# Queries before keys and values, keys and values between the attention blocks, decode beside the output projection

## The chip, the cores and the metric

The program runs on one core of a Trainium2 chip. A core has a matrix engine (TensorE, in profiles PE, its weight loads PEld), three engines that work on 128 partitions in parallel (VectorE or DVE, ScalarE or ACT, GpSimd or POOL), and a queue that only issues transfers (SyncE or SP). They run side by side and wait for each other through semaphores. Data lies in device memory, in SBUF (128 partitions) or in PSUM (8 banks of 512 float32 a partition, the only place TensorE writes). The metric is the time of one execution on the device, in microseconds.

## The reference, cut to what matters

One step of a two-layer decoder over a prompt of 1024 tokens and 8 sample tokens, 1032 rows of width 1024, all in float32. Layer 0 is a gated linear recurrence (untouched here). After its FFN, keys and values are projected once and the second layer attends to them:

```python
x = x + swiglu_ffn(rmsnorm(x, norm_ffn[0]), ...)            # end of layer 0
k_sh, v_sh = split(rmsnorm(x, kv_norm) @ w_kv, 2)            # 1024 -> 2048, also outputs
q = rmsnorm(x, norm_mix[1]) @ w_q_b                          # 4 heads x 2 maps x 128
s = einsum(q, k) * scale + rel_bias[bucket(q_pos - k_pos)]   # prompt: causal, 8 blocks of 128
p = softmax(s);  a = p[map 0] - lam * p[map 1]
o = rmsnorm(a @ v, subln) * (1 - lam_init)                   # per head, 256 values
x = x + o @ w_out_b
x = x + swiglu_ffn(rmsnorm(x, norm_ffn[1]), ...)
```

The 8 sample tokens do the same over 256 cached keys and values each, which lie in pages that a page table names, and their own new ones.

## The kernel before, in words

Rows are held feature-major: `resid` (X) is 8 chunks of 128 features by 1032 tokens. Each float32 projection is done as three products of a rounded part and a rest: `split_product` (L647) issues hi*hi, lo*hi and hi*lo on TensorE. The operands are `act_hi` and `act_lo` (XH, XL, written by ScalarE and VectorE) and `w_hi` and `w_lo`, which GpSimd's `split` (L591) makes from a slab of 2048 columns a partition in `w_stage`. There is one stage buffer and there are two slots of slabs: SyncE's `slab` (L454) refills the stage when the last split is done (`w_split`), and a split begins when TensorE has retired the slot two slabs back (`w_used`). A slab feeds 144 products on 344 columns (three token tiles).

Between layer 0's FFN and layer 1's FFN the kernel runs in phases with a barrier of TensorE, ScalarE and VectorE between them (`barrier`, L453): "f0", "kv", "q", "attn", "dattn".
- Last down pair of the FFN (`add_pair`): VectorE adds 24 results to X, ScalarE squares each chunk, VectorE sums.
- `norm("kv")`: sums over partitions, reciprocal root, then VectorE scales each chunk (`act_whole`, L1678), ScalarE rounds it, VectorE takes the rest (`act_lo`, L1676). X is spilled to device memory, since its place is used.
- `kv_slabs`: 16 chunks of 128 key or value features; ScalarE copies them out of PSUM, TensorE turns them to token rows (`turn_chunk`), VectorE copies the rows, ScalarE's queue writes them out. All keys (`k_feat`) and values (`v_rows`) stay in SBUF.
- `projection("q")`: the spilled X comes back in part, is scaled with another gain and split again, 4 slabs.
- Attention: 4 heads by 8 query blocks, an item being one block of one head. TensorE runs scores one item ahead, values one item behind; VectorE makes logits with bias and their maximum, ScalarE exponentials, VectorE the difference of the two maps, TensorE turns it, ScalarE copies it (`a_tok`), TensorE multiplies by the values. Scores use PSUM banks 0 to 3, turned weights 4 and 5, values 6, turned rows 7. The order within an item is written out in `at_head` on each engine. The rows of a head are normalised one head later.
- Decode ("dattn"): each sample token's query is spread over partitions by TensorE; VectorE multiplies it with the first page of keys, GpSimd with the second; VectorE reduces both. Softmax, then 64 products of value pages (256 columns each) against a memset block of weight columns.
- Output projection: 24 groups over the first 6 chunks (`out_early`), then 24 over the last 2 (`out_late`), added to the reloaded X; chunks of the next FFN's operand follow (`finish_projection`).

Of the kernel before, what the change touches and what calls it, by code (L numbers as in the profile page):

```python
# [80 lines left out]
def build(nc, i, o):  # L81
    ctx = ExitStack()
    with ctx:
# [44 lines left out]
        VS = place("v_s", [P, DEC])  # L128
        FS = place("f_s", [P, DEC])
        DL = place("chunk_decay", [P, NB])  # L130
# [16 lines left out]
        w_hi = sem("w_hi")  # L147
        phase_done = sem("phase_done")
# [12 lines left out]
        x_back = sem("x_back")  # L161
# [3 lines left out]
        chunk_turned = sem("chunk_turned")  # L165
        proj_free = sem("proj_free")
        rows_ready = sem("rows_ready")
        chunk_kept = sem("chunk_kept")
        rows_out = sem("rows_out")
# [43 lines left out]
        woa_free = sem("woa_free")  # L213
        wob_full = sem("wob_full")
# [24 lines left out]
        at_qb = sem("at_qb")  # L239
# [12 lines left out]
        d_bias = sem("d_bias")  # L252
        d_prod = sem("d_prod")
        dq_full = sem("dq_full")
        d_products = sem("d_products")
        d_products1 = sem("d_products1")
        dq_copied = sem("dq_copied")
        d_zeros = sem("d_zeros")
        d_orows = sem("d_orows")
        d_o_full = sem("d_o_full")  # L260
        d_a = sem("d_a")
        d_diag = sem("d_diag")
        d_o = sem("d_o")
        d_ss = sem("d_ss")
        d_rel = sem("d_rel")
# [3 lines left out]
        d_logit_full = sem("d_logit_full")  # L269
        d_bias_full = sem("d_bias_full")  # L270
        d_weights = sem("d_weights")
        d_a_full = sem("d_a_full")
        d_sq = sem("d_sq")
        d_ss_full = sem("d_ss_full")
        d_max = sem("d_max")
        d_exp = sem("d_exp")
        d_at = sem("d_at")
        d_ss_sum = sem("d_ss_sum")
        d_rstd = sem("d_rstd")
# [30 lines left out]


        S_HG, S_WOA, S_F0 = 0, 16, 21
        EARLY = 6
        S_K = S_F0 + 3 * NPAIR
        S_V, S_Q, S_WOB, S_F1 = S_K + 4, S_K + 8, S_K + 12, S_K + 17
# [6 lines left out]
        def part(name, shape, dt=F32):  # L322
# [33 lines left out]
        KT = part("k_feat", [P, C, SEQ])  # L356
        VTOK = part("v_rows", [P, NB, D])
        SF = at("kv_chunk", [P, T], F32, x_at)
        TKS = at("k_rows", [P, NB, P], F32, x_at + T * 4)
        TSS = at("kv_rows_sample", [DEC, P], F32, x_at + T * 4 + 4096)  # L360
        KV_CHUNKS = -(-(T * 4 + 4096 + P * 4) // (T * 4))
        QA = at("q_all", [P, C, T], F32, x_at)

        PB = [at(f"probs{s}", [P, 2, SEQ], F32, xh_at + s * 8192) for s in range(2)]
        BT = at("near_bias", [P, AH, 256], F32, xh_at + 16384)
        AT = at("a_tok", [P, NB, P], F32, xh_at + 20480)
        QB = [at(f"q_block{s}", [P, 2, P], F32, xh_at + 24576 + s * 1024) for s in range(2)]

        OT = ([at(f"o_tok{n}", [P, 256], F32, xh_at + 26624 + n * 1024) for n in range(6)]
              + [at(f"o_tok{n}", [P, 256], F32, rs_at + (n - 6) * 1024) for n in (6, 7)])  # L370
        OSQ = at("o_square", [P, 256], F32, rs_at + 2048)
        HK = at("hankel", [P, AH, 256], F32, xh_at + 8192)
        OH = at("onehots", [NBUCKET + 1, 384 + PAST + 1], F32, xh_at)
        RBX = at("rel_rows", [NBUCKET + 1, AH], F32, xh_at + 4096)
        DR = at("dist_vals", [AH, 384], F32, xh_at + 4352)


        empty = S_WOB % 2 ^ 1
        KPG = [[at(f"k_page{s}{g}", [P, D], F32, w_slots_at + (2 * s + empty) * SLAB * 4 + g * D * 4) for g in range(2)]
               for s in range(2)]  # L380
        VPG = [[at(f"v_page{s}{g}", [P, D], F32, arena + (4 + 2 * s + g) * 4096) for g in range(2)] for s in range(4)]
        KQP = [at(f"d_k_times_q{g}", [P, C, P], F32, xh_at + g * 4096) for g in range(NPG)]
        QBC = [at(f"d_q_all{s}", [P, C, P], F32, arena + s * 4096) for s in range(2)]

        WZ = at("d_weight_cols", [P, NPG, 32, 63], F32, xh_at + 8192)
        ORW = at("d_o_rows", [32, 256], F32, xh_at + 8192 + NPG * 32 * 63 * 4)
        d0 = arena + 12 * 4096
# [4 lines left out]
        DAT = at("d_a_tok", [P, 2, 64], F32, d0 + 4608)  # L392
        DDG = at("d_diag", [64, 64], F32, d0 + 5632)
# [9 lines left out]
        DST = at("d_stats", [64, 8], F32, d0 + 10880)  # L403

# [5 lines left out]
        PHASES = ["loaded", "f0", "kv", "q", "attn", "dattn"]  # L410
# [3 lines left out]
        SCALINGS = ["mix0", "woa", "ffn0", "kv", "q", "wob", "ffn1"]  # L414
        WHOLE = ["mix0", "kv", "q"]
        OLD = ["mix0", "kv"]
        LATE = ["ffn0", "ffn1"]
        PROJECTIONS = ["woa", "k", "v", "q", "wob"]
# [14 lines left out]
        AT_LATE = [(), (0, 1)] + [(n,) for n in range(2, NB)]  # L433
# [4 lines left out]

        def at_item(h, n, ahead):

            return h + (n + ahead) // NB, (n + ahead) % NB
# [11 lines left out]
        def _(sp):  # L453
# [62 lines left out]
            square(S_K, 8, i["w_kv"])  # L516
            square(S_Q, 4, i["w_q_b"][0])
            out_early(S_WOB, i["w_out_b"][0], 0, 1)

# [12 lines left out]
            for s in range(2):  # L532
                pages(kc, KPG, k_page_in, 0, s, s)
# [1579 lines left out]
```

## Time and profile before

| | us |
|---|---|
| median of 3 runs | 3135.26 (3132.32 to 3135.92) |
| profiled execution | 3135.91, span 3134.2 |
| TensorE busy in the span | 2867.7 (91%) |
| VectorE, ScalarE, GpSimd busy | 1300.4, 602.5, 923.0 |
| mean granted TensorE clock | 0.954 |

The span runs from the first to the last instruction of the profiled execution; what lies around it is 1.7 us. Busy times overlap between engines. A matmul's shown duration holds its way through the array too: one on 344 columns is shown as 326 ns, but the next starts 157 ns after it. Granted clock 1.00 is 2.4 GHz, 0.50 is 1.2 GHz.

### The profile page before, as it was taken

What the parts mean: (1) busy time and instruction counts of PE and PEld (TensorE: products, weight loads), DVE (VectorE), ACT (ScalarE), POOL (GpSimd) and SP (SyncE); (2) the same over time, 40 slices, a digit from 0 to 9 for tenths busy, and PEclk for the clock granted to TensorE, in tenths of its full rate; (3) what the DMA queues carried; (4) which work ended last, traced back from release to release, by engine and by line L of the source; (5) the groups of instructions that cost most, each with busy time, mean ns of one, the idle gap of its engine ahead of it and who ended that gap; (6) DMA issues with size and microseconds to landing.
All of it is one profiled execution on the core that took longest, in us unless ns stands there. A gap on an engine that the chain in (4) does not pass through costs nothing.

```text
span 3134.2 us, 43595 instructions
## 1 busy us (share of the span) xinstructions
PE 2867.7 (91%) x17823; PEld 2757.0 (88%) x17823; DVE 1300.4 (41%) x2092; ACT 602.5 (19%) x1113; POOL 923.0 (29%) x264
## 2 busy tenths in 40 slices
PE   5999999989899999999899796676698999999998
PEld 4999999989899999999799794444498999999998
DVE  6345555554433333333621305565234333333335
ACT  3122222212200000000221113453112000000003
POOL 3322222222343333334223320002133434333331
PEclk7999999989999999999999898897799999999999
DMA  3111111121111111111222201003311111111111
GB/s 95 40 43 51 54 55 56 42 89 42 41 41 54 41 54 41 54 41 48 88 75 81 95 24 35 0 0 122 141 51 41 41 54 41 54 41 54 41 54 55
DMA packets 196055, 170.23 MB, mean 54 GB/s; under 512 B 5514, under 2 KB 181373, under 8 KB 195502
## 3 DMA queue, kind: packets, MB, share of 16 engines
q1 hardware_dynamic: 157728, 132.20, 13.6%
q10 hardware_dynamic: 38158, 35.50, 3.4%
q8 instruction: 140, 2.29, 0.3%
q14 instruction: 29, 0.24, 0.0%
HBM read 142.35 MB, written 25.33 MB: 54 GB/s over the span
## 4 chain that ended last, share of the span: by engine, by line
PE 78%; issue 11%; DVE 8%; DMA 1%; POOL 1%; ACT 1%; SPq 0%; ACTq 0%; DVEq 0%; POOLq 0%
PE ps L649 23%; PE ps L651 23%; PE ps L650 23%; PE ps L860 3%; DVE act_whole L1678 1%; DVE hg_k L1763 1%; PE ps L1148 1%; DVE act_lo L1676 1%; DVE act_lo L1714 1%; DVE rstd L1693 1%; DMA k_page<-in_cache_k 1%; DVE hg_q L1762 1%; POOL d_k_times_q L633 1%; DVE act_lo L1698 1%; DVE act_whole L1641 0%
## 5 line engine op out<-in xcount | busy, mean ns | idle before, releaser
L649 PE MATMUL ps<-act_hi,w_hi 128*128 128x344 f32 x3840 | 1253.7, 326 | 71.9 <-DVE act_lo L1676 48.5
L650 PE MATMUL ps<-act_lo,w_hi 128*128 128x344 f32 x3840 | 1237.3, 322 | 0.0
L651 PE MATMUL ps<-act_hi,w_lo 128*128 128x344 f32 x3840 | 1237.0, 322 | 0.0
L597 POOL TENSOR_TENSOR w_hi<-w_stage,ones 128x2048 fp32r<-128x2048 f32 (+1 forms) x104 | 378.0, 3634 | 1520.9 <-PEq L701 1513.1
L649 PEld LDWEIGHTS ps<-act_hi,w_hi 128*128 128x128 f32 x3840 | 731.4, 190 | 81.2 <-issue 56.8
L650 PEld LDWEIGHTS ps<-act_lo,w_hi 128*128 128x128 f32 x3840 | 731.4, 190 | 1.7 <-issue 1.0
L651 PEld LDWEIGHTS ps<-act_hi,w_lo 128*128 128x128 f32 x3840 | 730.9, 190 | 0.0
L599 POOL TENSOR_TENSOR w_lo<-w_stage,w_hi 128x2048 fp32r<-128x2048 f32 (+1 forms) x104 | 477.0, 4587 | 8.2
L1878 DVE TENSOR_TENSOR resid<-resid,ps 128x344 f32<-128x344 f32 x528 | 270.6, 513 | 185.7 <-PE ps L651 185.2
L649 PE MATMUL ps<-h_hi,w_hi 128*128 128x344 f32 x1056 | 339.1, 321 | 1.4 <-DVE resid L1878 1.4
L651 PE MATMUL ps<-h_hi,w_lo 128*128 128x344 f32 x1056 | 338.3, 320 | 0.0
L650 PE MATMUL ps<-h_lo,w_hi 128*128 128x344 f32 x1056 | 338.1, 320 | 0.0
L1855 DVE TENSOR_TENSOR ps<-ps,rstd 128x344 f32<-128x344 f32 x132 | 68.9, 525 | 391.4 <-PE ps L651 391.4
L1858 DVE TENSOR_TENSOR ps<-ps,rstd 128x344 f32<-128x344 f32 x132 | 69.3, 525 | 363.2 <-PE ps L651 363.2
L1428 ACT ACTIVATE silu_gate<-ps 128x344 f32<-128x344 f32 x132 | 60.4, 458 | 807.7 <-DVE ps L1855 807.7
L649 PEld LDWEIGHTS ps<-h_hi,w_hi 128*128 128x128 f32 x1056 | 198.8, 188 | 4.5 <-DVE resid L1878 4.2
L650 PEld LDWEIGHTS ps<-h_lo,w_hi 128*128 128x128 f32 x1056 | 198.7, 188 | 0.0
L651 PEld LDWEIGHTS ps<-h_hi,w_lo 128*128 128x128 f32 x1056 | 198.6, 188 | 0.0
L1433 ACT CAST h_hi<-ps 128x344 fp32r<-128x344 f32 x132 | 59.0, 447 | 445.8 <-DVE ps L1861 445.8
L860 PEld LDWEIGHTS ps<-hg_q,hg_k 128*128 128x128 f32 x896 | 111.3, 200 | 25.9 <-DVE hg_k L1763 25.1
L860 PE MATMUL ps<-hg_q,hg_k 128*128 128x64 f32 x896 | 113.9, 282 | 20.9 <-DVE hg_k L1763 20.9
L1083 PE MATMUL ps<-v_rows,a_tok 128*128 128x256 f32 (+1 forms) x288 | 78.4, 422 | 44.1 <-ACT a_tok L1511 44.0
(251 smaller groups left out, 2234.2 us busy)
## 6 DMA issues: line engine op xcount, KB each, us to landing
w_stage<-in_w_gate_up SPq DMA_DIRECT2D x88, 512.0 KB, 5.0
w_stage<-in_w_down SPq DMA_DIRECT2D x44, 512.0 KB, 4.2
w_stage<-in_w_in_a SPq DMA_DIRECT2D x32, 512.0 KB, 5.2
w_stage<-in_w_kv SPq DMA_DIRECT2D x16, 512.0 KB, 4.3
k_page<-in_cache_k SPq DMA_DIRECT2D x16, 512.0 KB, 4.5
v_page<-in_cache_v SPq DMA_DIRECT2D x16, 512.0 KB, 4.8
x_spill<-resid ACTq DMA_DIRECT2D x1, 4128.0 KB, 11.2
resid<-x_spill ACTq DMA_DIRECT2D x1, 4128.0 KB, 12.5
```

Source lines behind the costliest of these rows:

```text
L597: g.tensor_tensor(WH[s][:, 0:cols], WST[:, 0:cols], ones[:, 0:1].to_broadcast([P, cols]), ALU.mult).then_inc(w_hi, 1)
L599: g.tensor_tensor(WL[s][:, 0:cols], WST[:, 0:cols], WH[s][:, 0:cols], ALU.subtract).then_inc(w_split, 1)
L649: pe.matmul(out, wh, xh, start=first, stop=False)
L650: pe.matmul(out, wh, xl, start=False, stop=False)
L651: return pe.matmul(out, wl, xh, start=False, stop=last)
L860: last = pe.matmul(PS[:, 3 + l % 2, c * 64:(c + 1) * 64], K[h % 2][:, c * P:(c + 1) * P], q[:, c, :, 1, :], start=True, stop=True)
L1083: last = pe.matmul(PS[:, 6, 0:256], AT[:, j, :], VTOK[:, j, bass.ds(h * 256, 256)], start=(j == 0), stop=(j == n))
L1428: a.activation(SIL[:, tile(t)], PS[:, t, 0:TS], ACT.Silu).then_inc(ffn_silu, 1)
L1433: a.copy(HH[par][:, k, tile(t)], PS[:, 3 + t, 0:TS]).then_inc(ffn_hh, 1)
L1855: v.tensor_tensor(PS[:, t, 0:TS], PS[:, t, 0:TS], RS[:, tile(t)], ALU.mult).then_inc(ffn_gscaled, 1)
L1858: v.tensor_tensor(PS[:, 3 + t, 0:TS], PS[:, 3 + t, 0:TS], RS[:, tile(t)], ALU.mult).then_inc(ffn_uscaled, 1)
L1878: v.tensor_tensor(X[:, m, tile(t)], X[:, m, tile(t)], PS[:, 6 + q % 2, 0:TS], ALU.add).then_inc(ffn_down_free, 1)
```

## The change

It takes all the phases but the first away, with their barriers, and writes the middle of the program in another order.
- After layer 0's FFN the raw residual is split once, `act_hi` and `act_lo` (`finish_first`, `out_rest` in `add_pair`). The gains of the two norms are multiplied into the weight slabs by GpSimd (a third pass in `split`, 12 slabs), and the reciprocal root is multiplied into the results by VectorE as it takes them out of PSUM (`q_take`, `kv_take`). So queries, keys and values share one operand.
- The queries come first: 4 slabs, written over X, whose chunks are spilled one by one.
- Keys and values are made by head and by token tile of 384, 384 and 264 columns: 48 groups of 24 products. Four stand ahead of attention, the others at set places between its items (tables `FILL_A`, `FILL_B`), each followed by the turn of the group before. Only two heads of keys and values are held.
- Attention's PSUM: scores in banks 3 to 6, turned weights in 3 and 4 as well, values in 7, turned rows and turned keys in 2, key/value groups in 0 and 1. Scores of an item now wait for the copy of the turned weights of two items back. Its output rows are written over the queries.
- The output projection has 24 whole groups of 24 products with the same token tiles (the 8 of the last tile come last); the decode steps stand between them. Both page products are VectorE's; the sum over the second page is 8 ScalarE copies with accumulation. The value pages are the stationary operand, with one moving column each: 128 products.

```diff
+                if gain is not None:
+                    w3 = WST[:].rearrange("p (k n) -> p k n", k=C)
+                    g.tensor_tensor(w3, w3, vec(gain).unsqueeze(2).to_broadcast([P, C, 256]), ALU.mult).then_inc(w_scaled, 1)
...
+        LATE_ROWS = [(), (0, 1)] + [(n,) for n in range(2, NB)]
+        LAST_ROWS = [(), (0, 1, 2), (3, 4, 5), (6, 7), (), (), (), ()]
+        FILL_A = [(4,), (6,), (8,), (10,), (), (12,), (13,), (15,)]
+        FILL_B = [(5,), (7,), (9,), (11,), (), (), (14,), ()]
+        WOB_TILES = ([(s, 2 * s + m, t) for s in range(4) for m in range(2) for t in range(2)]
+                     + [(s, (2 * s + m) % C, 2) for s in range(2, 6) for m in range(2)])
...
-            barrier(pe, "f0")
-            norm("kv", XH32)
...
+            first_slab("kv", S_Q % 2, q_full, (ffn_down_full, 24 * NPAIR + OPENED), sums_at=4)
...
+            def kv_turn(g):
...
+                pe.wait_ge(kv_free, g + 1)
...
+                    pe.wait_ge(kv_rows, g)
+                pe.wait_ge(at_o, rows_turned[0] + OPENED)
...
+            def at_scores(i):
...
+                pe.wait_ge(kv_free, 12 * h + 4 * (n // 3) + 2)
+                pe.wait_ge(at_logits, i + OPENED)
+                if i:
+                    pe.wait_ge(at_at, i - 1 + OPENED)
...
+            for item in range(AH * NB):
+                h, n = item // NB, item % NB
+                if item + 1 < AH * NB:
+                    at_scores(item + 1)
+                if n == 4:
+                    retire(kv_full, 12 * (h + 1))
+                for g in fills(FILL_A, h, n):
+                    kv_fill(g)
+                if item:
+                    at_values(item - 1)
+                at_turn_weights(item)
+                for g in fills(FILL_B, h, n):
+                    kv_fill(g)
...
+                if h:
+                    for m in late_rows(h)[n]:
+                        at_turn_rows((h - 1) * NB + m)
...
+            dq_spread(0)
+            dq_spread(1)
+            for w in range(24):
+                wob_group(w)
+                if w < 6:
+                    dq_spread(w + 2)
+                elif w == 8:
+                    d_logits()
+                elif w == 10:
+                    d_turn_weights()
+                elif w == 11:
+                    for b in range(4):
+                        d_values(b)
+                elif w == 13:
+                    for b in range(4, DEC):
+                        d_values(b)
...
+            ffn("f1", S_F1)
...
+                if w in (4, 8, 18, 20, 22):
+                    retire(wob_full, w)
...
+            page_scores(0)
+            wob_rest(6)
+            wob_rest(7)
+            page_scores(1)
```

The order on VectorE in attention, second head, where the logits of its fourth block (block 3) are made. Names: `probs` is what logits, exponentials and weights are made in, `o_tok` or `q_all` the attention rows, `k_feat` a key chunk. Before:

```order
L1944 TENSOR_SCALAR probs_125<-ps,far_bias 128x2x256
L1946 SCALAR_TENSOR_TENSOR probs_125<-ps,near_bias 128x256 x2
L1951 TENSOR_REDUCE stats<-probs_125 128x2
L1972 COPY o_tok_131<-ps 128x256
L1958 RECIPROCAL stats<-stats 128x1
```

After:

```order
L2041 TENSOR_SCALAR probs<-ps,far_bias 128x2x256
L2043 SCALAR_TENSOR_TENSOR probs<-ps,near_bias 128x256 x2
L2047 TENSOR_REDUCE stats<-probs 128x2
L2027 TENSOR_TENSOR k_sample<-ps,rstd 128x8
L2028 TENSOR_TENSOR k_feat_118<-ps,rstd 128x256
L2070 COPY q_all<-ps 128x2x128
```

The take of a key group stands between the maximum of an item and the rows and weights that follow it.

VectorE again, from the last down pair of layer 0's FFN on. `act_hi_scratch` holds the squares. Before, the last adds with their sums, and the first scaled chunks:

```order
L1878 TENSOR_TENSOR resid<-resid,ps 128x344
L1668 TENSOR_TENSOR act_hi_scratch<-act_hi_scratch 128x688
L1668 TENSOR_TENSOR act_hi_scratch<-act_hi_scratch 128x1032
L1678 SCALAR_TENSOR_TENSOR act_whole<-resid,vectors,rstd 128x1032 x2
L1676 TENSOR_TENSOR act_lo<-act_whole,act_hi 128x1032
```

After:

```order
L1779 TENSOR_TENSOR act_lo<-resid,act_hi 128x1032
L1961 TENSOR_TENSOR resid<-resid,ps 128x344 x3
L1779 TENSOR_TENSOR act_lo<-resid,act_hi 128x1032 x2
L1774 TENSOR_TENSOR rstd<-rstd,squares 128x1032 x5
L1996 TENSOR_TENSOR q_all<-ps,rstd 128x344 x6
```

The rests of the operand have moved among the adds, and the takes of the queries follow the sums with nothing between.

The third place is VectorE at the start of decode. `d_k_times_q` is a page of keys times the spread query. Before:

```order
L2025 COPY d_rel_rows<-d_rel 33x32 x2
L2033 TENSOR_TENSOR d_k_times_q_155<-k_page_143,d_q_all_157 128x1024
L2038 TENSOR_REDUCE d_scores_tok<-d_k_times_q_155 128x4x2
L2038 TENSOR_REDUCE d_scores_tok<-d_k_times_q_156 128x4x2
L2033 TENSOR_TENSOR d_k_times_q_155<-k_page_145,d_q_all_158 128x1024
```

After:

```order
L2137 TENSOR_TENSOR d_k_times_q_145<-k_page_133,d_q_all_147 128x1024
L2137 TENSOR_TENSOR d_k_times_q_146<-k_page_134,d_q_all_147 128x1024
L2142 TENSOR_REDUCE d_scores_tok<-d_k_times_q_145 128x4x2
L2085 TENSOR_TENSOR act_lo<-q_all,act_hi 128x1024 x2
L2137 TENSOR_TENSOR d_k_times_q_145<-k_page_135,d_q_all_148 128x1024
```

The last two rests of the output projection's operand stand behind the first page, whose two products are both here, and adds of the projection stand between the later pages.

## Rows read from the trace of the kernel before

**Rows 1.** Stages: stretch, its length, busy time (instructions) of each engine, clock, DMA

```profile
core 0: us, PE busy (x) PEld busy (x) DVE busy (x) ACT busy (x) POOL busy (x), PEclk, DMA share, GB/s
1545.90:1581.80 35.90, 17.59 (x60) 14.20 (x60) 27.99 (x19) 14.47 (x14) 9.67 (x2) 0.67 0.36 147
1581.80:1771.70 189.90, 189.36 (x1242) 188.21 (x1242) 23.64 (x47) 32.13 (x72) 57.43 (x14) 1.00 0.26 81
1771.70:1797.30 25.60, 8.65 (x37) 7.92 (x36) 16.07 (x10) 3.16 (x3) 9.66 (x2) 0.67 0.24 83
...
1886.20:1905.00 18.80, 4.85 (x12) 2.76 (x13) 4.21 (x13) 2.31 (x8) 0.00 (x0) 0.61 0.42 144
1905.00:2143.20 238.20, 170.37 (x663) 114.31 (x662) 145.61 (x297) 112.56 (x323) 0.00 (x0) 0.89 0.00 1
2143.20:2154.00 10.80, 4.65 (x16) 2.44 (x16) 2.79 (x10) 8.08 (x22) 0.00 (x0) 0.65 0.00 0
2154.00:2204.30 50.30, 23.07 (x128) 21.81 (x128) 33.38 (x32) 8.10 (x8) 27.12 (x8) 0.60 0.62 210
...
2255.00:2383.50 128.50, 119.37 (x728) 116.80 (x729) 55.28 (x70) 24.66 (x26) 46.78 (x12) 0.96 0.17 54
```

**Rows 2.** The chain of waits: start, length, what. A key turn; the reload

```profile
1588.69 0.87 PE ps L1021 x8
...
1776.14 6.11 DMA resid<-x_spill
```

**Rows 3.** Timeline, attention's last items: start, us, engine, line, operation, [idle before]

```profile
2123.65 1.81 DVE L1944 TENSOR_SCALAR probs<-ps,far_bias 128x1536 f32<-128x1536 f32 x1
2125.38 0.74 DVE L1946 SCALAR_TENSOR_TENSOR probs<-ps,near_bias 128x256 f32<-128x256 f32 x2
...
2126.16 2.29 DVE L1951 TENSOR_REDUCE stats<-probs 128x2 f32<-128x2048 f32 x1
...
2128.48 1.15 ACT L1501 ACTIVATE probs<-probs,stats 128x1024 f32<-128x1024 f32 x1 [5.04 <-DVE stats L1951]
...
2131.39 1.28 DVE L1963 SCALAR_TENSOR_TENSOR probs<-probs,stats 128x1024 f32<-128x1024 f32 x1
...
2132.15 5.29 PE L1083 MATMUL ps<-v_rows,a_tok 128*128 128x256 f32 x14 [5.34 <-ACT a_tok L1511]
...
2139.47 3.72 PE L1083 MATMUL ps<-v_rows,a_tok 128*128 128x256 f32 x16 [0.94 <-ACT a_tok L1511]
```

**Rows 4.** Stages again: a stretch of nothing but split products

```profile
1400.00:1450.00 50.00, 50.00 (x320) 49.98 (x319) 20.08 (x40) 4.06 (x9) 16.45 (x4) 1.00 0.15 43
```

**Rows 5.** One line (min/median/max ns), and the timeline of VectorE and GpSimd there

```profile
L1676 DVE TENSOR_TENSOR act_lo<-act_whole,act_hi x2: 1221/2926/4630, 1561.1 to 1571.1; 128x1032 fp32r<-128x1032 f32 x2
...
1565.66 5.55 DVE L1678 SCALAR_TENSOR_TENSOR act_whole<-resid,vectors,rstd 128x1032 f32<-128x1032 f32 x1
...
1560.38 4.28 POOL L597 TENSOR_TENSOR w_hi<-w_stage,ones 128x2048 fp32r<-128x2048 f32 x1 [29.90 <-PEq L701]
```

**Rows 6.** Timeline, ScalarE at the end of attention

```profile
2152.81 1.15 ACT L1533 ACTIVATE act_whole<-ps,lam 128x128 f32<-128x128 f32 x4 [0.32 <-PE ps L1092]
```

**Rows 7.** Timeline, decode: spreads cold and warm, page product, value pages; last, layer 0

```profile
2154.04 4.21 PE L1123 MATMUL ps<-ident,q_all 128*128 128x128 f32 x18 [0.75 <-ACTq L448]
...
2158.96 1.23 DVE L2033 TENSOR_TENSOR d_k_times_q<-k_page,d_q_all 128x1024 f32<-128x1024 f32 x1
...
2164.82 2.05 PE L1123 MATMUL ps<-ident,q_all 128*128 128x128 f32 x16 [0.48 <-ACT d_q_all L1572]
...
2210.83 29.73 PE L1148 MATMUL ps<-v_page,d_weight_cols 128*32 128x256 f32 x128 [0.83 <-DVE d_a_new_sum L2055]
...
705.37 1.84 PE L886 MATMUL ps<-hg_q,state_sample 128*128 128x1 f32 x16
```

**Rows 8.** Timeline, GpSimd: a slab split beside VectorE's adds from PSUM

```profile
2308.34 3.60 POOL L597 TENSOR_TENSOR w_hi<-w_stage,ones 128x2048 fp32r<-128x2048 f32 x1 [10.66 <-PEq L701]
2312.02 4.62 POOL L599 TENSOR_TENSOR w_lo<-w_stage,w_hi 128x2048 fp32r<-128x2048 f32 x1
```

**Rows 9.** Timeline, TensorE: the sum of squares in the next FFN's first slab

```profile
2368.18 2.08 PE L665 MATMUL ps<-rstd,ones 128*128 128x512 f32 x2 [8.24 <-DVE rstd L1693]
```

More of the change, by code:

```diff
@@ new lines, in _ @@
+            sp.wait_ge(v_out[0], 16 * 12)
+            sp.wait_ge(kv_turned, 36)
+            for b in range(2):
+                pages(kc, KPG, k_page_in, b, b)
+            columns(S_WOB + 2, w_out_b, 512)
+            for b in range(2, DEC):
+                sp.wait_ge(pg_scored, b - 1 + OPENED)
+                pages(kc, KPG, k_page_in, b, b % 2)
+            sp.wait_ge(at_av_full, AH * NB + OPENED)
+            sp.wait_ge(v_out[1], 16 * 12)
+            for b in range(2):
+                pages(vc, VPG, v_page_in, b, b)
@@ new lines, in d_turn_weights, with d_new_rows @@
+            def d_turn_weights():
+                pe.wait_ge(d_dve, D_DVE["weights"])
+                for g in range(NPG):
+                    pe.transpose(PS[:, 5, g * 64:(g + 1) * 64], DLG[:, g * P:(g + 1) * P], ident[0:64, 0:64])
+                pe.wait_ge(d_dve, D_DVE["diag"])
+                pe.matmul(PS[:, 6, 0:64], ones[0:64, :], DDG[:], start=True, stop=True).then_inc(d_pe, 1)
+            def d_new_rows(s):
+                for m in range(C):
+                    last = pe.transpose(PS[0:DEC, 3 + 2 * s + m // 4, (m % 4) * P:(m % 4 + 1) * P], (KS, VSF)[s][:, m, :], ident[:])
+                last.then_inc(new_turned, 1)
@@ new lines, in d_half @@
+            def d_half(b):
+                act.wait_ge(d_products, b + 1)
+                for m in range(C):
+                    r = m % 2 * 32 + m // 2 * DEC + b
+                    last = a.activation(KQP[1][:, m, :], KQP[1][:, m, :], ACT.Copy, accum_out=STS[:, 1, r:r + 1])
+                last.then_inc(d_halves, 1)
+            act.wait_ge(k_out[0], 16 * 12)
+            act.wait_ge(k_out[1], 16 * 12)
+            dq_copy(0)
+            dq_copy(1)
+            x_reload(6)
+            x_reload(7)
@@ new lines, in _ @@
+            a.copy(DAN[:], PS[:, 6, 0:64]).then_inc(d_act, 1)
+            act.wait_ge(new_turned, 2)
+            for s in range(2):
+                last = a.copy(RWS[s][:].rearrange("p (u n) -> p u n", u=2), PS[0:DEC, 3 + 2 * s:5 + 2 * s, :])
+            last.then_inc(new_rows, 1)
+            act.wait_ge(d_dve, D_DVE["o"])
+            a.activation(DSQ[:], DO[:], ACT.Square).then_inc(d_act, 1)
+            act.wait_ge(d_pe, D_PE["ss_full"])
+            a.copy(DSQ[:].rearrange("p c b -> p (c b)"), PS[:, 3, 0:64]).then_inc(d_act, 1)
@@ L1943, in at_logit @@
                 if near:
-                    v.tensor_scalar(PB[n % 2][:, :, 0:near], both[:, :, 0:near], SCALE, c31[:, bass.ds(h, 1)], ALU.mult, ALU.add)
-                for c in range(2):
-                    last = v.scalar_tensor_tensor(out=PB[n % 2][:, c, near:width], in0=both[:, c, near:width], scalar=SCALE,
-                                                  in1=BT[:, bass.ds(h, 1), 256 - (width - near):256].squeeze(1),
-                                                  op0=ALU.mult, op1=ALU.add)
@@ L1967, in at_rows @@
-            def at_rows(h, n, turned):
-                dve.wait_ge(at_av_full, h * 8 + n + 1 + OPENED)
-                if turned:
-                    dve.wait_ge(at_ot_turned, (h - 1) * 8 + n + 1 + OPENED)
-                v.tensor_copy(OT[n][:], PS[:, 6, 0:256]).then_inc(at_ot, 1)
+                    v.tensor_scalar(pb[:, :, 0:near], both[:, :, 0:near], SCALE, c31[:, h:h + 1], ALU.mult, ALU.add)
+                for e in range(2):
+                    last = v.scalar_tensor_tensor(out=pb[:, e, near:width], in0=both[:, e, near:width], scalar=SCALE,
+                                                  in1=BT[:, h, 256 - (width - near):256], op0=ALU.mult, op1=ALU.add)
```

976 lines of the change are left out of this document (509 added, 467 removed).

## The prediction

> **What bounds the kernel now.** TensorE carries most of this kernel, so a gain can only come from stretches where it waits or does avoidable work. The table by stage [rows 1] finds them: one long stretch, 1545.9 to 2383.5 us, in which TensorE's share changes from stage to stage. The key/value stage runs at 189.4 busy of 189.9; the joints around it are half empty (17.6 of 35.9, 8.7 of 25.6, 4.9 of 18.8); attention is busy 170.4 of 238.2 at a granted clock of 0.89, while GpSimd is idle; and 50.3 us of decode beside it run at 0.60. A busy TensorE in attention is 170.4 x 0.89 = 152 us of work at full clock.
>
> The chain of waits says why the joints are empty [rows 2]: after the last down product a normalisation and 16 VectorE passes over the residual, and later its reload. In attention the idle times before each operation [rows 3] name the loop between VectorE and ScalarE; its largest item costs VectorE 1.81 + 0.74 + 2.29, ScalarE 2.3 and VectorE about 1.8 before the next logits: 9.0 us, against 3.4 + 3.4 + 0.9 of TensorE. So in attention TensorE is idle because of that loop, and independent products would fit there.
>
> **Unit prices.** A split product on 344 columns is 0.157 us (320 in 50 us [rows 4]); by columns 384 take 0.175 and 264 take 0.121, so a group of 24 is 4.2 or 2.9 us and three groups are 11.3, as now. If a product had a floor at today's 0.157, the 264-column ones would cost 0.9 us a group more: 14 us over the 16 groups and 7 over the other 8. I take the proportional price, since the 128x128 turns run at 0.109 each, 8 in 0.87 [rows 2].
>
> **Part 1, into the queries.** Now: 1545.9 to 1581.8. After: the rounding and rest of each chunk of the raw residual follow its last add, so the first query slab starts behind the down products. Per chunk VectorE has 3 x 0.51 + 1.15 = 2.7 us against TensorE's 2.83; the two sums of squares in that stretch put 1.5 us over. The sum matmuls stay (1.9 us), the distance matmul waits for VectorE's sixth take (1.5 us).
>
> Here a cost comes in that no edit names: **GpSimd against VectorE**. A VectorE operation that reads two operands from SBUF takes 1.22 us alone and 4.63 or 5.55 beside a slab split, whose first pass takes 4.28 [rows 5] instead of 3.60 [rows 8]: one waits for the other's end. Adds that read PSUM are not of that kind: the split of 3.60 ran beside them. In the down stage the rests now meet two splits and the new scaling pass: 3 us; the five sums of squares meet a third: 1.5 us. First query slab at 1545.9 + 1.5 + 3 = 1550.4; queries 576 x 0.157 = 90.6, + 1.9 + 1.5 + 1.5 = 95.5, end 1645.9. The scaling pass (about 3.6 to 4.6 us of GpSimd) hides: a slab then needs 5 + 4.6 + 8.2 = 18 us of DMA and GpSimd, TensorE 22.6 for a query slab; without that cover, 12 slabs would each pay.
>
> The page "GPSIMD Engine Reference" of the Trainium skill, section "Specifications", goes further than these rows: it says that VectorE instructions in a two-port mode contend as well. That would include the scaling of the attention rows, which run now with GpSimd idle, so no row here shows it. By that rule I would add some 3 us; by the rows nothing.
>
> **Part 2, attention with keys and values between.** Work: 152 (attention) + 1152 x 0.157 = 181.2 (same columns) + 128 turns x 0.11 with their starts = 16: 349 us. What TensorE still waits for, item by item with the durations of [rows 3]:
> - block 4 has no fill. Scores of block 5 end; then VectorE 2.0 + 1.75, ScalarE 1.95 + 0.6 + 0.7 and hand-overs: 7.5 us until the weights of item 4 are copied, which the next scores now await because the turned weights lie in score banks. TensorE has 3.2 us to do: 4.3 idle.
> - block 5 1.3, block 7 0.9, by the same count with one fill of 4.5 us.
> - where a row turn follows a key turn in bank 2, 0.8 (blocks 1, 2, 3, 6), and 1.0 for the second row of block 1.
> That is 6.5 us for head 0, 10.7 each for heads 1 and 2. The last head has no fills in blocks 4 to 7: 4.4 + 5.2 + 5.5 + 2, and three rows at a time in blocks 1 to 3: 6.4; together 23.5. Sum 51. Idle times of over 5 us cost clock: after 5.34 us of idling, 14 instructions took 5.29 us where 16 take 3.72 [rows 3]; 6 us for the last head. GpSimd now splits 8 slabs under attention: its 24 passes mostly meet VectorE when a fill covers it; 4 us. One more for the first value slab. 349 + 51 + 6 + 4 + 1 = 411: end of the last values 2056.9, against 2143.2 now.
>
> **Part 3, tail of attention.** Now 10.8 us [rows 1] to the last turned row. After: six reloads issued by ScalarE before the row factors, put at 2.2 in all, make it 13.0. Then the first spread at half clock (18 in 4.21 us [rows 7], so 3.7), its copy 1.0, two page products at 1.23 [rows 7], a reduce of the same length, and only then the last two rests, 2.3: 23.7 us. The output projection begins at 2080.9 (now 2255.0).
>
> **Part 4, decode beside the output projection.** To the end of the next FFN's first slab (now 2383.5): 576 products 90.6; six spreads at 2.05 [rows 7] 12.3; the value pages: now 128 instructions, 29.7 us; after 256 with one moving column, at 1.84 us for 16 [rows 7] 29.4; small matmuls 5; cold start 2; the first slab with its sums 24.5. VectorE and ScalarE need about 5.7 us a page (2.5 products, 8 accumulating copies estimated at 0.39 from the 0.29 pitch of [rows 6] and a read), under TensorE's 6.25. GpSimd's split of the third slab blocks the page products: 5 us. Then slab supply: a slab is split only when its slot is free, takes 3.60 + 4.62 us [rows 8], and stages some 5.2 us after the previous split. The tail groups use 5.8 us a slab, so TensorE waits 3.5 + 8.5 + 8 = 20, and 3 more where the sums of squares stretch the splits. Sum: 90.6 + 12.3 + 29.4 + 5 + 2 + 24.5 + 5 + 20 + 3 = 191.8, end 2272.5.
>
> The 8.2 us wait for the sum of squares in that first slab [rows 9] goes: the sums are ready when the slab starts.
>
> **Sum.** 2383.5 - 2272.5 = 111 us off the profiled execution's 3135.9 (span 3134.2), 0.6 above the median of the runs: **3025 us**.
>
> **Rivals.**
> 1. *Fills add instead of filling.* ScalarE's and VectorE's queues are in order; if a take or key copy always waits for TensorE's fill, attention keeps its 238 us plus 5 at its start and the key/value work comes on top: 243 + 197 = 440 of 411, and 10 for blocked passes: +39, 3064 us. For it: each take stands ahead of the weights in VectorE's order. Against: in blocks 0 to 3 the loop is under 8.6 us and TensorE's item over 10.
> 2. *The clock stays at 0.89*, as in attention now. 349 / 0.89 = 392, +43, less the 6 counted: 3062. Against: gaps in fewer than a quarter of the items reach 4 us.
> 3. *Slower than before.* The turned weights now share banks 3 and 4 with the scores; if by that sharing each item becomes one serial chain (scores, logits, exponentials, copy, values), engines add: 152 + 145.6 + 112.6 [rows 1] + 197 = 608 instead of 411: 3226. It decides over 522 us for the merged stage. Against: the next scores wait only for a copy, and the weights are made an item ahead.
> 4. *Faster:* the page loop and slab supply overlap better, or the joins of banks cost half: 51 + 20 + 5 halved is 38 off: 2987.
> That the order isn't as said is excluded: it is written out, instruction by instruction.
>
> **Chances.** Forecast 0.60 (3003 to 3047), rival 1 0.14, rival 2 0.08, rival 4 0.12, rival 3 0.03, others 0.03. The floor price of small products (+21) lies between forecast and rival 1. The range leaves out the slow end beyond rival 1 and half of rival 4: 2990 to 3064. A change under 0.2% (6 us) can't be told from none here: faster 0.95, same 0.01, slower 0.04.
>
> **What the profile of after would show.** Right: split products without a gap from the down stage into the queries; merged stage of about 411 us at a clock near 1, waits on the copied weights of some 4 us once a head and 5 in the last head's end; 24 us with little TensorE before the output projection; waits on GpSimd's low halves at the last three slabs. VectorE's weights step beside a split stretched by up to 4 us. Wrong: TensorE waiting in every item, half-clock stretches between fills, or page products taking more than 6 us a page, which would move time into the first six groups.

## Result: 3066 us, where 3025 was forecast

The changed kernel takes 3066.39 us (median of 4 runs, 3061.58 to 3068.63), the kernel before 3135.08 beside it: ratio 0.978, 95% interval 0.9763 to 0.9797. So it is faster, by 69 us and not by 110, 2 us beyond the slow end of the range. The profiled execution has a span of 3066.8 us against 3134.2; the first FFN slab of layer 1 ends at 2316.1 (before 2383.5), forecast 2272.5. That leaves 43.6 us to find.

The table by stage of the kernel after; columns as in [rows 1]. Its boundaries are the start of GpSimd's split of the first query slab, the first query product, the first key product, the end of the last values of attention, the first output product, and the end of that FFN slab:

```profile
core 0: us, PE busy (x) PEld busy (x) DVE busy (x) ACT busy (x) POOL busy (x), PEclk, DMA share, GB/s
1523.79:1558.55 34.76, 26.11 (x143) 24.69 (x142) 25.34 (x32) 14.16 (x14) 11.81 (x3) 0.90 0.36 138
1558.55:1662.51 103.96, 96.39 (x586) 92.88 (x585) 33.03 (x35) 7.35 (x9) 49.08 (x12) 0.97 0.15 52
1662.51:2075.56 413.05, 363.93 (x1952) 308.54 (x1952) 209.54 (x376) 133.66 (x353) 97.85 (x24) 0.95 0.16 49
2075.56:2099.73 24.17, 10.33 (x49) 7.98 (x49) 9.05 (x19) 12.08 (x26) 0.00 (x0) 0.71 0.36 135
2099.73:2316.10 216.37, 190.96 (x1126) 186.94 (x1127) 97.65 (x88) 58.30 (x177) 55.28 (x13) 0.84 0.30 103
```

The same last down pair in the kernel before, from the start of the split to the end of the last down product:

```profile
1522.16:1545.90 23.74, 23.72 (x143) 22.08 (x141) 18.45 (x35) 7.50 (x7) 8.23 (x2) 1.00 0.14 46
```

| step of the forecast | forecast | measured | excess |
|---|---|---|---|
| all before that split (untouched code) | 0 | 1523.79 - 1522.16 | 1.6 |
| down stage to first query product | 23.7 + 4.5 | 34.8 | 6.5 |
| queries | 95.5 | 104.0 | 8.5 |
| merged stage | 411 | 413.1 | 2 |
| tail | 24.0 | 24.2 | 0.2 |
| output projection with decode, first FFN slab | 191.6 | 216.4 | 24.8 |

The largest edit, keys and values between the items of attention, came out as forecast. The misses are in the two joints.

**Joint one.** VectorE and GpSimd in the timeline of after:

```profile
1523.79 3.60 POOL L610 TENSOR_TENSOR w_hi<-w_stage,ones 128x2048 fp32r<-128x2048 f32 x1 [4.52 <-PEq L698]
1527.47 4.61 POOL L612 TENSOR_TENSOR w_lo<-w_stage,w_hi 128x2048 fp32r<-128x2048 f32 x1
1538.00 3.60 POOL L607 TENSOR_TENSOR w_stage<-w_stage,vectors 128x2048 f32<-128x2048 f32 x1 [5.93 <-DMA w_stage<-in_w_q_b]
1558.95 3.60 POOL L610 TENSOR_TENSOR w_hi<-w_stage,ones 128x2048 fp32r<-128x2048 f32 x1 [17.35 <-PEq L698]
1562.64 5.48 POOL L612 TENSOR_TENSOR w_lo<-w_stage,w_hi 128x2048 fp32r<-128x2048 f32 x1
1573.29 4.53 POOL L607 TENSOR_TENSOR w_stage<-w_stage,vectors 128x2048 f32<-128x2048 f32 x1 [5.17 <-DMA w_stage<-in_w_q_b]
```

```profile
1529.71 3.46 DVE L1779 TENSOR_TENSOR act_lo<-resid,act_hi 128x1032 fp32r<-128x1032 f32 x1
...
1535.33 1.23 DVE L1779 TENSOR_TENSOR act_lo<-resid,act_hi 128x1032 fp32r<-128x1032 f32 x1
...
1538.71 3.98 DVE L1779 TENSOR_TENSOR act_lo<-resid,act_hi 128x1032 fp32r<-128x1032 f32 x1
...
1559.18 10.02 DVE L1779 TENSOR_TENSOR act_lo<-resid,act_hi 128x1032 fp32r<-128x1032 f32 x2
1569.13 9.78 DVE L1774 TENSOR_TENSOR rstd<-rstd,squares 128x1032 f32<-128x1032 f32 x5
```

A rest takes 1.23 us alone, and 3.46 and 3.98 where GpSimd is in a pass: each ends 1.1 us after that pass (1533.17 after 1532.08, 1542.69 after 1541.60), so nearly all of its work of 1.23 us comes behind the pass. The scaling pass at 1538.00 is the change's own. TensorE, in the same timeline:

```profile
1544.32 0.66 PE L648 MATMUL ps<-h_hi,w_hi 128*128 128x344 f32 x1 [4.17 <-DVE resid L1961]
1544.77 0.49 PE L649 MATMUL ps<-h_lo,w_hi 128*128 128x344 f32 x1
...
1578.97 2.07 PE L664 MATMUL ps<-rstd,ones 128*128 128x512 f32 x2 [6.10 <-DVE rstd L1774]
```

The down products have two banks, so an add behind a stretched rest stops TensorE within one group. The products after the wait of 4.17 us come 0.286 us apart instead of 0.157.

**Joint two.** TensorE in decode: the value products, and the granted clock in slices of 5 us (columns: stretch, length, PE busy, clock, DMA share, GB/s):

```profile
2165.71 22.48 PE L1172 MATMUL ps<-d_a_sum,v_page 128*128 128x1 f32 x128
...
2198.11 24.01 PE L1172 MATMUL ps<-d_a_sum,v_page 128*128 128x1 f32 x128
```

```profile
2165.00:2170.00 5.00, 5.00 (x46) 1.00 0.05 17
2170.00:2175.00 5.00, 5.00 (x30) 0.60 0.67 211
2175.00:2180.00 5.00, 5.00 (x25) 0.50 0.66 210
...
2190.00:2195.00 5.00, 5.00 (x26) 0.85 0.53 203
2195.00:2200.00 5.00, 5.00 (x37) 1.00 0.00 0
2200.00:2205.00 5.00, 5.00 (x33) 0.67 0.01 3
2205.00:2210.00 5.00, 5.00 (x25) 0.50 0.00 0
```

The profile shows no idle time of TensorE here, and yet its clock falls from 2.4 to 1.2 GHz, twice. After the first block it comes back while split products run; after the second it is back at 2225.4, behind the turns of the new rows. The page "TensorE: Matmul & The Clock Gate" of the Trainium skill, section "HAM oscillation — how this bites in real kernels", looks for lost clock in gaps in which TensorE is idle; these rows have none, so by that rule nothing would be lost here, and the rows decide.

The waits behind the second block; the last three are those for slabs:

```profile
2238.88 0.36 PE L648 MATMUL ps<-act_hi,w_hi 128*128 128x264 f32 x1 [4.67 <-DVE act_lo L2203]
2256.37 0.59 PE L648 MATMUL ps<-act_hi,w_hi 128*128 128x264 f32 x1 [4.09 <-POOL w_lo L612]
2270.45 0.59 PE L648 MATMUL ps<-act_hi,w_hi 128*128 128x264 f32 x1 [6.50 <-POOL w_lo L612]
2286.74 0.63 PE L648 MATMUL ps<-act_hi,w_hi 128*128 128x344 f32 x1 [8.87 <-DVE act_lo L1791]
```

Two of the three end with GpSimd's low pass (the second pass of a split, which makes `w_lo`), as forecast. The third doesn't: that slab's low pass ended at 2285.49, and TensorE waited 1.1 us more for VectorE's rest, which took 5.54 us beside it.

### The profile page after: what moved, and what is told of

Read it like the earlier page. It is cut to its first block, busy times and chain, and to the rows that moved or that the text cites. A ratio compares the mean times of both kernels' runs of the same rounds, so it can differ in the third digit from the quotient of the medians.

```text
span 3066.8 us, 43328 instructions
## 1 busy us (share of the span) xinstructions
PE 2871.7 (94%) x17949; PEld 2783.2 (91%) x17949; DVE 1322.3 (43%) x2077; ACT 585.0 (19%) x1157; POOL 956.9 (31%) x270
## 4 chain that ended last, share of the span: by engine, by line
PE 85%; DVE 8%; issue 3%; ACT 2%; POOL 1%; PEld 0%; ACTq 0%; DMA 0%; SPq 0%; DVEq 0%; PEldq 0%; POOLq 0%
PE ps L648 24%; PE ps L650 23%; PE ps L649 23%; PE ps L843 3%; PE ps L1067 3%; PE ps L1087 2%; PE ps L1172 2%; DVE hg_k L1846 1%; DVE rstd L1774 1%; DVE act_lo L1779 1%; DVE stats L2047 1%; DVE hg_q L1845 1%; DVE act_lo L1791 1%; PE ps L1135 1%; DVE act_whole L1731 1%
## 5 line engine op out<-in xcount | busy, mean ns | idle before, releaser
L648 PE MATMUL ps<-act_hi,w_hi 128*128 128x344 f32 (+2 forms) x3840 | 1262.8, 329 | 55.4 <-DVE act_lo L1757 15.2
L649 PE MATMUL ps<-act_lo,w_hi 128*128 128x344 f32 (+2 forms) x3840 | 1238.0, 322 | 0.0
L650 PE MATMUL ps<-act_hi,w_lo 128*128 128x344 f32 (+2 forms) x3840 | 1237.5, 322 | 0.0
L612 POOL TENSOR_TENSOR w_lo<-w_stage,w_hi 128x2048 fp32r<-128x2048 f32 (+1 forms) x105 | 488.2, 4650 | 8.3
L1067 PE MATMUL ps<-k_feat,q_all 128*128 128x512 f32 (+3 forms) x192 | 81.1, 565 | 27.9 <-ACT a_tok L1552 27.3
```

What stands on the lines that cost most here:

```text
L612: g.tensor_tensor(WL[s][:, 0:cols], WST[:, 0:cols], WH[s][:, 0:cols], ALU.subtract).then_inc(w_split, 1)
L648: pe.matmul(out, wh, xh, start=first, stop=False)
L649: pe.matmul(out, wh, xl, start=False, stop=False)
L650: return pe.matmul(out, wl, xh, start=False, stop=last)
L1067: last = pe.matmul(PS[:, bank + k0 // 512, 0:k1 - k0], QA[:, 2 * h + c, n * P:(n + 1) * P], KTB[h % 2][:, c, k0:k1], start=True, stop=True)
```

## Experiments

Each is the changed kernel with one edit, unless said otherwise. Executions of one kernel differ by up to 15 us, and a profiled one can be any of them (for the changed kernel, hold split and three edits it is the slowest, for page moving the fastest). So I compare medians and, in the profiled executions, lengths between landmarks: A from the start of the low pass of the first query slab to the first key product (135.0 in the changed kernel), B from there to the start of the last values (409.3), C from the first output product to the sum of squares in the FFN slab (197.3 in the first profiled execution, 200.5 in the second).

| kernel | median us | ratio, 95% | A | B | C |
|---|---|---|---|---|---|
| changed | 3066.4 | 0.978 (0.9763 to 0.9797) | 135.0 | 409.3 | 197.3 |
| changed, again | 3068.4 | 0.9788 (0.9772 to 0.9804) | 135.1 | 409.3 | 200.5 |
| hold both | 3057.4 | 0.9761 (0.9745 to 0.9777) | 121.6 | 409.3 | 200.3 |
| hold split | 3064.3 | 0.9773 (0.9757 to 0.9789) | 125.9 | 418.6 | 200.3 |
| no scaling | 3061.5 | 0.9774 (0.9747 to 0.9801) | 125.7 | 409.1 | 200.3 |
| eight columns | 3067.0 | 0.9789 (0.9772 to 0.9805) | 134.8 | 409.5 | 200.5 |
| interleaved values | 3081.1 | 0.9834 (0.9818 to 0.9851) | 135.0 | 409.4 | 213.9 |
| page moving | 3049.3 | 0.9737 (0.9716 to 0.9757) | 135.1 | 409.4 | 176.6 |
| new rows late | 3062.9 | 0.977 (0.9748 to 0.9792) | 135.1 | 409.4 | 203.3 |
| fills at once | 3162.9 | 1.0088 (1.0064 to 1.0111) | 135.2 | 508.3 | 200.3 |
| three edits | 3030.9 | 0.9664 (0.965 to 0.9678) | 121.7 | 412.5 | 176.4 |
| three edits, rows on ScalarE | 3029.8 | 0.9668 (0.9654 to 0.9681) | 121.7 | 409.4 | 176.6 |

### Who blocks whom in joint one

`norm_acc` counts VectorE's sums of squares, and the edit lets GpSimd begin with the second query slab only behind the last of them:

```diff
                 pool.wait_ge(w_staged, n * 32 + 32)
+                if n == S_Q + 1:
+                    pool.wait_ge(norm_acc, (nth("kv") + 1) * (C - 1))
                 if gain is not None:
```

> GpSimd starts on the second query slab (scaling and split) only when the seven sums of squares after layer 0's FFN are made; nothing else differs from the changed kernel (3066.4 us). Theory A: the missing 12 us of the joint come from VectorE operations with SBUF operands that wait for GpSimd's passes while adds, and so PSUM banks and TensorE, queue behind them. Then the wait of 4.17 us for a residual add goes (with 18 products at 0.286 instead of 0.157, 2.3 us), and so does the wait of 6.10 us for the sums with about 1 us of lower clock behind it: about 13 us, 3053 us. Rival B: the rests themselves (1.23 us each) in VectorE's queue ahead of the adds are what TensorE waits for: at most 3 us, 3064. Rival C: the slab held back comes too late for TensorE (it has 22.6 us for the first slab): slower, 3070 or more.

A got 13.4 us shorter, the median 9 (where 13 was expected). The held kernel by stage, and VectorE and GpSimd there:

```profile
1520.15:1550.24 30.09, 23.92 (x143) 22.23 (x142) 22.41 (x32) 14.16 (x14) 8.21 (x2) 1.00 0.41 159
1550.24:1645.45 95.21, 93.74 (x586) 91.62 (x585) 22.24 (x35) 7.36 (x9) 50.89 (x13) 1.00 0.17 57
```

```profile
1553.60 6.58 DVE L1776 TENSOR_TENSOR rstd<-rstd,squares 128x1032 f32<-128x1032 f32 x5
...
1560.32 3.60 POOL L609 TENSOR_TENSOR w_stage<-w_stage,vectors 128x2048 f32<-128x2048 f32 x1 [31.88 <-DVE rstd L1776]
```

Five sums take 6.58 instead of 9.78 us, the clock is 1.00 in both stretches, and the queries take 95.2 us, where the forecast had 95.5. TensorE doesn't miss the slab that starts late: that GpSimd made it early was worth nothing. Theory A stands. What remains in the down stage is the first slab's own split under the first rest and the rests themselves: 30.1 us against 23.7.

The same wait one step later, ahead of the split and behind the scaling pass:

> As the kernel that holds back both, but only the split of the second query slab waits for the sums; its scaling pass stays at 1538, under the last down pair. Theory A: the scaling pass keeps its own 4.17 + 2.3 us, the rest goes: about 7 us, 3059. If the new third pass is all of the contention that matters, nothing goes: 3066. If the split is, as much goes as with both held: 3053.

A is 9.2 us shorter. So of 13.4 us the one scaling pass at 1538 carries 4.2, and GpSimd's work beside the last rests and the sums 9.2. But the median fell by 2 only, and B shows where it went: 409.3 became 418.6. B grows in two steps, of 4.8 us in the second head and 5.8 in the third. The beginning of the first step, at the weights of the second head's sixth block (block 5), VectorE and then GpSimd:

```profile
1816.65 4.45 DVE L2063 SCALAR_TENSOR_TENSOR probs<-probs,stats 128x768 f32<-128x768 f32 x1
1821.02 4.66 DVE L2082 TENSOR_SCALAR q_all<-q_all,row_factor 128x256 f32<-128x256 f32 x1
```

```profile
1813.01 3.60 POOL L607 TENSOR_TENSOR w_stage<-w_stage,vectors 128x2048 f32<-128x2048 f32 x1 [5.12 <-DMA w_stage<-in_w_kv]
1816.68 3.60 POOL L612 TENSOR_TENSOR w_hi<-w_stage,ones 128x2048 fp32r<-128x2048 f32 x1
1820.36 5.16 POOL L614 TENSOR_TENSOR w_lo<-w_stage,w_hi 128x2048 fp32r<-128x2048 f32 x1
```

The next logits start at 1825.60 with no idle time before them. In the changed kernel the weights of that item took 1.02 us, and the row scaling fell beside a pass too, but VectorE was idle for 1.94 us behind it:

```profile
1830.52 1.02 DVE L2061 SCALAR_TENSOR_TENSOR probs<-probs,stats 128x768 f32<-128x768 f32 x1
1831.45 3.69 DVE L2080 TENSOR_SCALAR q_all<-q_all,row_factor 128x256 f32<-128x256 f32 x1
```

A row scaling takes 0.34 us elsewhere and reads one operand from SBUF. The forecast counted only operations with two such operands. It had set aside the page "GPSIMD Engine Reference" of the Trainium skill, section "Specifications", by which VectorE instructions in a two-port mode contend too. The trace agrees as far as this operation goes, with 3.69 and 4.66 us; which mode it runs in, it doesn't show. Which operation meets which pass depends on when each starts, so this B holds for the profiled execution, the slowest of the four (3068.3 us); the fastest took 3057.3, which is what A alone would give.

The scaling pass left out for all 12 slabs (`if gain is not None` never taken), so that the gains are missing from the results:

> GpSimd's scaling pass is left out for all 12 slabs of queries, keys and values, so that the gains of the two norms are missing from these results; nothing else changes. Theory A: the pass isn't hidden, because VectorE's operations on SBUF wait for its end: the wait of 4.17 us in the last down pair with its half clock (2.3) goes, of the 9.78 us of the five sums about 3, and some 4 us of attention, where row factors and weights meet it: 13 us, 3053. Rival B: only the low and high passes matter, and they stay: 3064 to 3066.

A is 9.3 us shorter, B the same (409.1). So the third pass costs at the joint, where the scaling passes at 1538 and 1573 are, and in this execution nothing in attention; the 4 us I expected there were not there. The median is 5 us lower, but the intervals overlap.

### Why the value products run at half clock

```diff
...
-                                         DAS[:, g, r:r + 1], start=(g == 0), stop=(g == NPG - 1))
+                                         DAS[:, g, r:r + 1].to_broadcast([P, 8]), start=(g == 0), stop=(g == NPG - 1))
```

> Each value product of the decode streams its weight column eight times (eight moving columns, seven results unused); the number of products and weight loads is the same. Now the 128 of a block take 22.48 and 24.01 us at a granted clock that falls from 1.00 to 0.50 some 4 us into each block, where 16 in 1.84 us would give 14.7. Theory A: the clock falls because TensorE multiplies too little in these blocks, and eight times as many columns keep it up: about 17 us off in the blocks and 3 behind them, 3046. Rival B: eight columns are still too few or it is the dense run of weight loads that does it: the same time, 3066, the same clock of 0.50.

Nothing changed: blocks of 23.09 and 22.94 us, the clock down to 0.50 in both, the median 3067.0. Eight moving columns run as one does.

```diff
+                    if 12 <= w < 15:
+                        j = C * (w - 12) + k
+                        for q in range(8 * j // 3, 8 * (j + 1) // 3):
+                            value_pair(q)
...
```

> The value products are not two blocks but stand two or three pairs at a time between the split products of three output groups; same products, same operands. Theory A: it takes a run of several us of one-column products to lower the clock (16 of them between other products ran in 1.84 us at 1.00 in layer 0): the clock stays at 1.00 and about 17 us go in the products and 3 behind them: 3046. Rival B: the share of one-column products decides (about 30 us of them beside 12.6 us of others), the clock falls all the same and now takes the three groups with it: 3070.

Worse, by 15 us. That is rival B, who expected 4. TensorE's clock stays down through all three groups:

```profile
2165.00:2170.00 5.00, 5.00 (x33) 0.74 0.00 0
2170.00:2175.00 5.00, 5.00 (x23) 0.50 0.69 213
...
2240.00:2245.00 5.00, 5.00 (x24) 0.75 0.00 0
```

The split products between them ran at half clock too. So it isn't the length of one run of value products. The third test changes the form:

```diff
-                for m in range(C):
-                    r = m // 2 * DEC + b
+                for h in range(AH):
                     for g in range(NPG):
-                        last = pe.matmul(PS[:, 7, m * DEC + b:m * DEC + b + 1], VPG[b % 4][g][:, m * P:(m + 1) * P],
-                                         DAS[:, g, r:r + 1], start=(g == 0), stop=(g == NPG - 1))
+                        last = pe.matmul(PS[0:32, 7, 0:256], WZ[:, g, h * DEC + b, :], VPG[b % 4][g][:, 256 * h:256 * (h + 1)],
+                                         start=(b == h == g == 0), stop=(b == DEC - 1 and h == AH - 1 and g == NPG - 1))
...
```

`WZ` is a zeroed block of 32 x 32 columns for each page half, with the weights on its diagonal; GpSimd clears it once, and two more products turn the result.

> The value products of the decode in the form of the kernel before: the page is the moving operand (256 columns), 32 weight columns the stationary one, 64 products instead of 128, and their row result is turned behind group 14 (two turns more); groups and all else stay. Before the change the same products took 29.73 us at a granted clock of 1.00; now 46.5 us, mostly at 0.50. Theory A: the clock in this stretch falls because of the form with one moving column (eight did not help, and mixing them with split products took these down too): it stays at 1.00, 17 us go in the products and 3 behind them: 3047. Rival B: the clock falls there for another reason (what ran before, the transfers of the value pages beside it): 0.50 again, and 256 moving columns then cost twice 29.7: 3080.

Both blocks and the clock in them:

```profile
2162.89 14.00 PE L1177 MATMUL ps<-v_page,d_weight_cols 128*32 128x256 f32 x64
...
2185.42 14.00 PE L1177 MATMUL ps<-v_page,d_weight_cols 128*32 128x256 f32 x64
```

```profile
2165.00:2175.00 10.00, 10.00 (x48) 1.00 0.57 183
2185.00:2195.00 10.00, 10.00 (x48) 1.00 0.00 0
```

28.0 instead of 46.5 us, C at 176.6, the median 17 us lower. Theory A stands: in the same place, beside the same transfers, the form with one moving column loses the clock and the one with 256 doesn't. What in the form does it stays open. The 64 products have 256 moving columns, but also weights of 32 columns instead of 128 and half as many weight loads, and no run parts these; forms between 8 and 256 moving columns were not tried.

### Is it the order that fills?

```diff
-        FILL_A = [(4,), (6,), (8,), (10,), (), (12,), (13,), (15,)]
-        FILL_B = [(5,), (7,), (9,), (11,), (), (), (14,), ()]
+        FILL_A = [(4, 5, 6, 7, 8, 9, 10, 11), (), (), (), (), (12, 13, 14, 15), (), ()]
+        FILL_B = [(), (), (), (), (), (), (), ()]
```

> The same groups, turns and items as in the changed kernel (3066.4 us), in another order: of each head, eight key/value groups stand in one row in block 0 and the four of the next head in one row in block 5; no other block has a fill. Theory A: the groups between the items are what fills the idle time of attention. Without them the items wait as before the change, where attention had 238.2 - 170.4 = 68 us of idle time and a clock of 0.89; the merged stage, now 413 us, gets 20 to 30 us longer: 3086 to 3096 us. Rival B: the gain came from the barriers and joints that went, and TensorE's work would take as long in either order: within 5 us, 3061 to 3071.

Both theories missed: the merged stage takes 512 us, 99 more, and the kernel is slower than the one before the change. The stage, two of the waits in the first head, and all waits of the scores for the copy in this stage, here and in the changed kernel (us in total, times, longest):

```profile
1662.55:2174.54 511.99, 399.57 (x1952) 325.73 (x1952) 197.90 (x376) 132.19 (x353) 94.96 (x24) 0.88 0.12 40
```

```profile
1721.96 3.75 PE L1067 MATMUL ps<-k_feat,q_all 128*128 128x512 f32 x4 [2.57 <-ACT a_tok L1552]
...
1752.33 6.06 PE L1067 MATMUL ps<-k_feat,q_all 128*128 128x512 f32 x8 [4.06 <-ACT a_tok L1552]
```

```profile
PE ps L1067 <- ACT a_tok L1552: 67.7, 25, 5.0
```

```profile
PE ps L1067 <- ACT a_tok L1552: 27.3, 11, 4.5
```

I took attention's old idle time, 68 us, for what the fills cover. But scores now share banks with the turned weights and wait for their copy; without a fill that wait is open, in 25 items for 67.7 us instead of in 11 for 27.3. Of the 99 us, 63.3 are idle time (112.4 instead of 49.1), 40.4 of them this wait, and 35.7 are longer busy time at a clock of 0.88 instead of 0.95. So the mechanism that rival 3 names is at work, though not as one serial chain (608 us); the forecast had it decide at 522 us, and this kernel is 10 us short of it. The fills cover the wait in the changed kernel. A kernel with separate banks for scores and weights was not run, so the price of the sharing by itself isn't shown.

### The rest, and a faster version

> The 16 turns of the new key and value rows (1.87 + 1.91 us) move from behind the second block of value products to behind the sum of the decode rows' squares, into the wait of 4.67 us for the samples' operand. Theory A: they fill that wait: 3.5 us off, 3063. Rival B: the chain through ScalarE's two table loads starts no earlier than now, or the turns delay it: no change, 3066.

The edit moves `d_new_rows(0)` and `d_new_rows(1)` behind `d_sums()` on TensorE, with ScalarE's copies. The wait fell from 4.67 to 2.92 us, the turns took 1.04 + 1.04 instead of 1.87 + 1.91, since the clock was back by then. But now split products stand behind the second block, and they run at 0.50 in the turns' place. From the end of that block to the sum of squares it is 76.5 us, against 74.9 and 76.8 in the two profiled executions of the changed kernel. The median is 3.5 us lower, but the intervals overlap: not settled, and the traces show no gain.

> The changed kernel as it is, once more, beside the two that follow. Its executions so far lie between 3061.6 and 3068.6 us. Theory A: GpSimd's 24 passes in the merged stage meet VectorE's operations by chance of timing (in the run that held only the split, the stage had the same program and 9.3 us more than in the changed kernel's profiled run, in two steps of 4.8 and 5.8 us): the median comes within 5 us of 3066 and the executions differ by 5 us or more, where the kernel before, with GpSimd idle in attention, should differ less. Rival B: that stage is as steady as in the kernel before; its executions stay within 3 us.

Not settled either: 3060.6 to 3072.6 in 5 executions, against 3128.0 to 3136.1 in 9 of the kernel before. Both spread, and B was 409.3 as before, so the expected meetings by chance within one kernel didn't show in it. Of the spread, some 8 us arise in layer 0, in code that is the same in all these kernels: in their twelve profiled executions the low pass of the first query slab began between 1519.4 and 1527.5 us.

> Three edits together, each measured alone: GpSimd waits for the sums before the second query slab (13 us between the landmarks, 9 in the median), the page as moving operand (20.5 us between the landmarks, 17 in the median), the new rows' turns behind the decode sums (3.5). If they are independent, 30 to 37 us off 3066: 3029 to 3036. If a gain in front is taken back by another meeting of GpSimd and VectorE in attention, as with the split held alone: up to 9 us more, 3040.

3030.85 us, 0.9664 of the kernel before. The two large savings add (13.3 in A, 21 to 24 in C), and B lost 3. The third edit adds nothing that shows: C is 176.4 us, and with page moving alone it was 176.6.

> As the kernel with three edits, but in attention ScalarE multiplies the attention rows by their factor (24 passes of 128x256 over SBUF) instead of VectorE; the last head's stay on VectorE. On VectorE one takes 0.34 us, but 3.69 or 4.66 beside a pass of GpSimd, ahead of the next item's logits. Theory A: those meetings go, the merged stage gets 4 to 9 us shorter and the executions closer to each other: 3022 to 3029 where the three edits give 3033. Rival B: ScalarE's exponentials and copies are in the loop, and about 0.4 us more a block makes them late: 5 us slower, 3038. Rival C: other operations of VectorE (weights, 4.2 to 4.8 us beside a pass) meet them instead: the same, 3033.

B went from 412.5 to 409.4, which is what the three edits had lost there, and the medians can't be told apart (3030.9 and 3029.8): rival C, with 3 us at most. The weights, stretched in the same way, stay on VectorE.

## Why the prediction was wrong, by its steps

- **"Where GpSimd against VectorE" in part 1: 3 us for the rests, 1.5 for the sums.** The mechanism was named, its size was not. Of 15.0 us excess in the joint, holding GpSimd back gave 13.4. I counted too few meetings. On VectorE the stretches add to 15.7 us (2.2, 2.8 and 7.6 for the rests, 3.2 for the sums), and 4.5 were counted. Two rests under one split took 10.02 us ([rows 5] has 4.63 for one), which moved the sums into the next pass as well. And I didn't ask who is queued behind: adds, so banks, so TensorE within one group (4.17 us) and at the sums (6.10), and then the clock (0.50 and 0.55 for 5.3 and 5.5 us).
- **"The scaling pass hides."** It hides from TensorE's wait for slabs, which was the only cover I looked at. It doesn't hide from VectorE: one such pass cost 4.2 us, and leaving all of them out saved 9.3.
- **"256 with one moving column, at 1.84 us for 16 [rows 7] 29.4."** The row was 16 between other products at a clock of 1.00. In blocks of 128 it is 46.5: 17.1 us, and some 3.3 in the turns and products behind. With the page moving it was 28.0.
- **"Cold start 2" in part 4.** Behind each of the waits of 4.09, 6.50 and 8.87 us some 5.5 us ran at 0.70, 0.73 and 0.65: 5 us more. The wait of 4.67 us for the samples' operand and one of 1.3 for the diagonal of new weights had no term.
- **Right in part 4:** 20 + 3 for slab supply measured 19.5, of which 1.1 is VectorE's rest; the price by columns held (24 products on 264 columns in 2.9 us), so there was no floor. The 5 us for blocked page products were not paid: two of them took 7.80 us beside a split, but TensorE didn't wait. 17.1 + 3.3 + 5 + 4.7 + 1.3 - 5 - 3.5 is 22.9 of the 24.8; 1.9 stay open.
- **Part 2 right, partly by luck:** 49.1 us of idle time against 51 + 5, but 363.9 us busy at 0.95 is 346 of work and 18 of clock, against 349 and 6. **Part 3 right:** 24.2 against 24.0 (its terms add to 23.7, and the forecast's ends are off by 0.3 us there and 0.2 in part 4).
- **Rivals.** 1 fell (413 us, no adding). 2 fell in its place (0.95, not 0.89), while the clock was lost where I had not looked. 3, whose own sum gives 3222 and not 3226, names a wait that is real but covered. No row stood behind the 4 us in the argument against 2: in these runs half clock followed waits of 4.17 us and up, while after one of 2.51 us the clock stayed at 1.00 in the changed kernel and was 0.50 in the one without scaling. 4 fell.

## What to carry to other kernels

When an operation that can wait for another engine's pass is moved into a queue, price the queue behind it, up to the engine that stops, not the operation. Take the price of a small product from a stretch that holds as many of them as the one you plan. A resource that is shared because there is cover, like these banks, is to be costed once without the cover, since that is what a later change of order will pay.

## What was not expected of the hardware

- TensorE's granted clock fell to 0.50 while it was busy without a gap, in products of 128x128 weights with one or eight moving columns (22.5 to 24.0 us a block instead of the 14.7 that 16 in 1.84 us give), and took split products mixed with them down too. The same data as moving operand, 256 columns on 32 of weights, ran at 1.00.
- A VectorE operation with one SBUF operand, 128x256, took 3.69 and 4.66 us beside a GpSimd pass, and 0.34 alone; one on 64x64, the diagonal of new weights, 4.52.
- Holding one split back changed, in the profiled execution, a stage that begins 75 us later by 9.3 us, through which operation met which pass.
